# Four SwiGLU FFNs whose first product is made in seven block products of half the tokens instead of eight

## The reference, cut to what matters

```python
def swiglu_2(x, w_gate, w_up, w_down):
    return (jax.nn.silu(x @ w_gate) * (x @ w_up)) @ w_down
def second_block(...):
    for l in range(DEPTH_2):        # 2
        x = layer_norm(ALPHA * x + 0.5 * swiglu_2(x, ffn1_gate[l], ffn1_up[l], ffn1_down[l]), ...)
        ...                         # pooling and HGRN2 mixer, layer norm
        x = layer_norm(ALPHA * x + 0.5 * swiglu_2(x, ffn2_gate[l], ffn2_up[l], ffn2_down[l]), ...)
```

## Time and profile before

| | us |
|---|---|
| median of 3 runs | 2878.31 (2878.22 to 2878.59) |
| profiled execution, its span | 2877.4 |
| PE busy | 2850.9 (99%) |
| DVE busy | 1219.8 (42%) |
| ACT busy | 1009.8 (35%) |
| POOL busy | 398.4 (14%) |

### The profile page before, as it was taken

How to read it: one execution, slowest core, us unless ns; L and a number is a source line. 1 busy time by engine, 2 the same in 40 slices (tenths; PEclk the granted TensorE clock), 3 DMA queues, 4 the chain that set the end, 5 groups by cost and what they waited for, 6 DMA issues and landing times.

```text
span 2877.4 us, 34540 instructions
## 1 busy us (share of the span) xinstructions
PE 2850.9 (99%) x14629; PEld 2357.3 (82%) x14629; DVE 1219.8 (42%) x1631; ACT 1009.8 (35%) x1400; POOL 398.4 (14%) x422
## 2 busy tenths in 40 slices
PE   9999999899999999999999999999999999999999
PEld 8888887678888888888888888888888888888887
DVE  5554343553342433334646333343333464633333
ACT  5233244652232332323344323233222343432222
POOL 0115616201110000010232000100001013200010
PEclk9999999999999999999999999999999999999999
DMA  4333223123333233332212333323333221233332
GB/s 150 100 98 95 91 75 93 53 81 96 98 99 96 88 95 97 101 93 84 86 62 81 96 95 98 94 87 95 97 100 93 84 89 60 81 96 95 96 95 81
DMA packets 77465, 262.11 MB, mean 91 GB/s; under 512 B 12224, under 2 KB 12352, under 8 KB 77312
## 3 DMA queue, kind: packets, MB, share of 16 engines
q1 hardware_dynamic: 77312, 259.91, 29.1%
HBM read 256.60 MB, written 2.10 MB: 90 GB/s over the span
## 4 chain that ended last, share of the span: by engine, by line
PE 95%; DVE 2%; ACT 2%; issue 1%; POOL 0%; ACTq 0%; DVEq 0%; POOLq 0%
PE bank L340 26%; PE bank L342 25%; PE bank L341 25%; PE bank L357 2%; PE bank L363 2%; PE bank L358 2%; PE bank L477 2%; PE bank L406 1%; PE bank L410 1%; PE bank L407 1%; PE bank L487 1%; PE bank L377 1%; PE bank L373 1%; PE bank L372 1%; PE bank L799 1%
## 5 line engine op out<-in xcount | busy, mean ns | idle before, releaser
L1409 DVE TENSOR_TENSOR wlo<-wraw,whi 128x1024 fp32r<-128x1024 f32 x473 | 594.5, 1268 | 853.6 <-ACT whi L896 853.0
L896 ACT ACTIVATE whi<-wraw 128x1024 fp32r<-128x1024 f32 x478 | 499.9, 1056 | 929.5 <-DMA wraw<-weights 928.3
L340 PE MATMUL bank<-Hh,whi 128*128 128x512 f32 x2104 | 822.2, 391 | 2.3 <-DVE wlo L1409 1.1
L342 PE MATMUL bank<-Hl,whi 128*128 128x512 f32 x2104 | 818.9, 389 | 0.0
L341 PE MATMUL bank<-Hh,wlo 128*128 128x512 f32 x2104 | 818.7, 389 | 0.0
L340 PEld LDWEIGHTS bank<-Hh,whi 128*128 128x128 f32 x2104 | 395.0, 188 | 85.6 <-issue 3.1
L342 PEld LDWEIGHTS bank<-Hl,whi 128*128 128x128 f32 x2104 | 394.9, 188 | 82.1
L341 PEld LDWEIGHTS bank<-Hh,wlo 128*128 128x128 f32 x2104 | 395.1, 188 | 81.2
L340 PE MATMUL bank<-Ah,whi 128*128 128x512 f32 x1056 | 412.7, 391 | 0.0
L342 PE MATMUL bank<-Al,whi 128*128 128x512 f32 x1056 | 411.0, 389 | 0.0
L341 PE MATMUL bank<-Ah,wlo 128*128 128x512 f32 x1056 | 410.8, 389 | 0.0
(11 more groups left out here) (310 smaller groups left out, 2605.7 us busy)
## 6 DMA issues: line engine op xcount, KB each, us to landing
wraw<-weights SPq DMA_DIRECT2D x478, 512.0 KB, 3.6
X<-x_t SPq DMA_DIRECT2D x8, 256.0 KB, 6.5
y_t<-X SPq DMA_DIRECT2D x8, 256.0 KB, 2.1
dist<-attention SPq DMA_DIRECT2D x4, 256.0 KB, 4.2
wraw<-weights SPq DMA_DIRECT2D x2, 256.0 KB, 3.9
Y<-masks SPq DMA_DIRECT2D x1, 512.0 KB, 8.6
zsum<-attention SPq DMA_DIRECT2D x2, 256.0 KB, 3.3
MUb<-attention SPq DMA_DIRECT2D x2, 256.0 KB, 3.5
```

Of the source, the lines that this page charges most:

```text
L340: pe.matmul(b, sh, mh, start=start, stop=False)
L342: signal(pe.matmul(b, sh, ml, start=False, stop=stop), keys)
L896: act.activation(whi[:, u % NS, :], wraw[:, u % NS, :], ACT.Copy).then_inc(*S.done("weights_hi", ("hi", u)))
L1409: dve.tensor_tensor(wlo[:, u % NS, :], wraw[:, u % NS, :], f32(whi[:, u % NS, :]), SUB).then_inc(*S.done("weights_lo", ("lo", u)))
```

## The change

In the four FFNs with a layer norm, the first group (j = 0, 1) stays as it was. The other ten pairs go by 2x2 blocks: tokens in two halves a and b of 256, contraction in k and k+4, hidden tiles j and j+1. Instead of eight block products, seven are made, from sums of weight tiles and sums of token blocks, and each result block is a sum of some of them (the scheme of Strassen and Winograd). Gate and up are done alike, as the two halves e of one bank. In detail:

- The weights of these groups leave the stream. A step (a pair unit, v) is eight tiles, k and k+4 by j and j+1 by gate and up, loaded as 512 KB into one of four slots praw of 16 tiles. POOL adds up 512, 256 and 256 columns to make eight more tiles (`pair_sums`); ACT makes the high parts of 14 of the 16 (phi, three slots), DVE the low parts in place (plo).
- POOL makes four sums of token blocks for each of four k, once an FFN (`token_sums`); ACT and DVE split them into TF.
- PE does 7 x 2 x 3 matmuls of 256 columns a step, four steps a group, into seven banks.
- DVE adds the seven banks up to the four blocks in cb (`blocks`), ACT takes silu of the gate halves in one operation, DVE multiplies both hidden tiles in one (`product`) into Af, in float32, which lies where Al will.
- Slots and TF lie in the place of Ah from tile 4 on. So only tiles 0 to 3 are split early; the other 18 are split in `late_a`, when the last step is done, and there POOL makes a third of the Al. The first two units of the second product's weights are loaded behind the third-last step, the next two behind the last one (`behind`).
- One unit of each second-block mixer is blank and not loaded.

```diff
+FIRST_TILES = 4 * KD
+PAIRED = ("a0", "b0", "a1", "b1")
+N_PAIRS = (NF // 2 - 1) * 4
...
+KEPT = 4
...
+def pair_plan():
+    plan = []
+    for l in range(2):
+        for n in (1, 2):
+            for j in range(2, NF, 2):
+                for k in range(4):
+                    for kk, jj in ((k, j + 1), (k + 4, j + 1), (k, j), (k + 4, j)):
+                        plan.extend((f"{m}{n}_{l}", kk, jj) for m in ("gate", "up"))
...
+    Al, o_al = ar("Al", [P, NF, T], F32R)
+    Af, _ = ar("Af", [P, NF, T], F32, o_al)
+    Ah, o_ah = ar("Ah", [P, NF, T], F32R)
+    o_t = o_ah + KEPT * T * 4
...
+        def pair_group(st, j):
+            v0 = PAIRED.index(st) * N_PAIRS + (j - 2) * 2
...
+            for k in range(4):
+                v = v0 + k
+                raw, hi = pair_slots(v)
+                products = ((4, H[:, :, k, half[0]], None), (6, H[:, :, 4 + k, half[0]], None), (2, TF[:, :, 3, k, :], 3),
+                            (12, TF[:, :, 1, k, :], 1), (10, TF[:, :, 2, k, :], 2), (8, TF[:, :, 0, k, :], 0),
+                            (14, H[:, :, 4 + k, half[1]], None))
+                for i, (t, both, form) in enumerate(products):
+                    b = open_bank((use, i), True) if k == 0 else bank((use, i))
+                    if i == 0:
+                        pe.wait_ge(*S.at(("pair lo", v)))
+                    if form == 3 and j == 2:
+                        pe.wait_ge(*S.at(("TF", st, k)))
+                    if i == 3:
+                        pe.wait_ge(*S.at(("sum lo", v)))
+                    for e in range(2):
+                        o = b[:, half[e]]
+                        pe.matmul(o, plo[raw][:, t + e, :], both[:, 0, :], start=k == 0 and e == 0, stop=False,
+                                  skip_group_check=True)
+                        pe.matmul(o, phi[hi][:, t + e - 2, :], both[:, 0, :], start=False, stop=False,
+                                  skip_group_check=True)
+                        ins = pe.matmul(o, phi[hi][:, t + e - 2, :], both[:, 1, :], start=False, stop=k == 3,
+                                        skip_group_check=True)
...
+        def pair_hi(v):
+            raw, hi_slot = pair_slots(v)
+            s = v % N_PAIRS
...
+            act.wait_ge(pair_in[raw], 16 * pair_landings(v))
...
+                act.wait_ge(*S.at(("pair unit", v - 3)))
+            act.activation(phi[hi_slot][:, 0:6, :], praw[raw][:, 2:8, :], ACT.Copy).then_inc(
+                *S.done("weights_hi", ("pair hi", v)))
+            act.wait_ge(*S.at(("sums", v)))
+            act.activation(phi[hi_slot][:, 6:14, :], praw[raw][:, 8:16, :], ACT.Copy).then_inc(
+                *S.done("weights_hi", ("sum hi", v)))
...
+        def ffn_pairs(st, arena_free, tmp_free):
...
+            for k in range(4):
+                act.wait_ge(*S.at(("T sums", st, k)))
+                act.activation(TF[:, 0, :, k, :], Tf[:, :, k, :], ACT.Copy).then_inc(*S.done("moving_hi", ("TF hi", st, k)))
+            pair_hi(v0)
+            pair_hi(v0 + 1)
...
+            for j in range(2, NF, 2):
+                for k in range(4):
+                    s = 2 * (j - 2) + k
+                    if 0 < s < N_PAIRS - 2:
+                        pair_hi(v0 + s + 2)
+                    elif s >= N_PAIRS - 2:
+                        hi(u0 + 4 + s - N_PAIRS + 2)
+                    if k == 0 and j > 2:
+                        silu_pair(st, j - 2)
...
+                    if k == 3:
+                        act.wait_ge(*S.at(("full", ((st, j), 0))))
+                        act.wait_ge(*S.at(("product", st, j - 1)))
+                        act.activation(cb[:, 0, :], bank(((st, j), 0))[:, :], ACT.Copy).then_inc(
+                            *S.done("rows_out", ("first product", st, j), empties=[((st, j), 0)]))
...
+        def split_a(st, j):
+            act.wait_ge(*S.at(("product", st, j)))
+            act.activation(Ah[:, j, :], Af[:, j, :], ACT.Copy).then_inc(*S.done("moving_hi", ("Ah", st, j)))
+        def late_a(st):
...
+            for j in range(KEPT, NF):
+                hi_to(p + j)
+                if j == NF - 4:
+                    silu_pair(st, NF - 2)
+                split_a(st, j)
...
+        def pair_lo(v):
+            raw, hi_slot = pair_slots(v)
+            dve.wait_ge(*S.at(("pair hi", v)))
+            dve.wait_ge(*S.at(("sums", v)))
+            dve.tensor_tensor(plo[raw][:, 2:8, :], praw[raw][:, 2:8, :], f32(phi[hi_slot][:, 0:6, :]), SUB).then_inc(
+                *S.done("weights_lo", ("pair lo", v)))
+            dve.wait_ge(*S.at(("sum hi", v)))
+            dve.tensor_tensor(plo[raw][:, 8:16, :], praw[raw][:, 8:16, :], f32(phi[hi_slot][:, 6:14, :]), SUB).then_inc(
+                *S.done("weights_lo", ("sum lo", v)))
...
+            for k in range(4):
+                dve.wait_ge(*S.at(("TF hi", st, k)))
+                dve.tensor_tensor(TF[:, 1, :, k, :], Tf[:, :, k, :], f32(TF[:, 0, :, k, :]), SUB).then_inc(
+                    *S.done("moving_lo", ("TF", st, k)))
+            pair_lo(v0)
...
+            for j in range(2, NF, 2):
+                for k in range(4):
+                    s = 2 * (j - 2) + k
+                    if 0 < s < N_PAIRS - 2:
+                        pair_lo(v0 + s + 2)
+                    elif s >= N_PAIRS - 2:
+                        lo(u0 + 4 + s - N_PAIRS + 2)
+                    if k == 0 and j > 2:
+                        product(st, j - 2)
...
+                    if k == 3:
+                        blocks(st, j)
+        def blocks(st, j):
...
+            c11, c12, c21, c22, u2 = cb[:, 0, :], cb[:, 1, :], cb[:, 2, :], cb[:, 3, :], tmp[4][:, :]
+            dve.wait_ge(*S.at(("first product", st, j)))
+            dve.wait_ge(*S.at(("full", ((st, j), 3))))
+            dve.tensor_tensor(u2, b(3), c11, ADD).then_inc(*S.done("blocks", ("u2", st, j), empties=[((st, j), 3)]))
+            dve.wait_ge(*S.at(("u2", st, j)))
+            dve.tensor_tensor(c11, b(1), c11, ADD).then_inc(*S.done("blocks", ("c11", st, j), empties=[((st, j), 1)]))
+            dve.wait_ge(*S.at(("full", ((st, j), 4))))
+            dve.tensor_tensor(c21, b(4), u2, SUB).then_inc(*S.done("blocks", ("w", st, j)))
+            dve.wait_ge(*S.at(("w", st, j)))
+            dve.tensor_tensor(c21, b(2), c21, ADD).then_inc(*S.done("blocks", ("c21", st, j), empties=[((st, j), 2)]))
+            dve.wait_ge(*S.at(("full", ((st, j), 5))))
+            dve.tensor_tensor(c12, b(5), u2, ADD).then_inc(*S.done("blocks", ("u4", st, j), empties=[((st, j), 5)]))
+            dve.wait_ge(*S.at(("u4", st, j)))
+            dve.tensor_tensor(c22, b(4), c12, SUB).then_inc(*S.done("blocks", ("c22", st, j), empties=[((st, j), 4)]))
+            dve.wait_ge(*S.at(("full", ((st, j), 6))))
+            dve.wait_ge(*S.at(("c22", st, j)))
+            dve.tensor_tensor(c12, b(6), c12, ADD).then_inc(*S.done("blocks", ("blocks", st, j), empties=[((st, j), 6)]))
+        def product(st, j):
+            dve.wait_ge(*S.at(("silu", st, j)))
...
+            dve.tensor_tensor(Af[:, j:j + 2, :].rearrange("p j (h t) -> p (j h) t", h=2), cb[:, :, HALF:T], cb[:, :, 0:HALF],
+                              MUL).then_inc(*S.done("gates", ("product", st, j), ("product", st, j + 1), *last))
...
+        def late_a(st):
+            for j in range(KEPT, NF):
+                lo_to(p + j)
+                if j == NF - 4:
+                    product(st, NF - 2)
+                if j % 3:
+                    split_a(st, j)
...
+        def pair_sums(v):
+            raw = praw[pair_slots(v)[0]]
+            pool.wait_ge(pair_in[pair_slots(v)[0]], 16 * pair_landings(v))
+            pool.tensor_tensor(raw[:, 8:12, :].rearrange("p (f e) n -> p f (e n)", f=2),
+                               raw[:, 2:6, :].rearrange("p (f e) n -> p f (e n)", f=2),
+                               raw[:, 0:2, :].rearrange("p e n -> p (e n)").unsqueeze(1).to_broadcast([P, 2, 2 * P]),
+                               ADD).then_inc(*S.done("pool_pairs", ("two sums", v)))
+            pool.wait_ge(*S.at(("two sums", v)))
+            pool.tensor_tensor(raw[:, 12:14, :], raw[:, 8:10, :], raw[:, 4:6, :], ADD).then_inc(
+                *S.done("pool_pairs", ("third sum", v)))
+            pool.wait_ge(*S.at(("third sum", v)))
+            pool.tensor_tensor(raw[:, 14:16, :], raw[:, 12:14, :], raw[:, 6:8, :], ADD).then_inc(
+                *S.done("pool_pairs", ("sums", v)))
+        def token_sums(st):
+            a, b = slice(0, HALF), slice(HALF, T)
+            for k in range(4):
+                pool.wait_ge(*S.at(row_done(st, k)))
+                if k == 0:
+                    pool.wait_ge(*S.at(row_done(st, 4)))
+                pool.wait_ge(*S.at(row_done(st, 4 + k)))
+                pool.tensor_tensor(Tf[:, 2, k, :], X[:, k, b], X[:, 4 + k, b], SUB).then_inc(
+                    *S.done("pool_pairs", ("T third", st, k)))
+                pool.tensor_tensor(Tf[:, 0, k, :], X[:, k, a], X[:, k, b], SUB)
```

(29 more changed lines are left out.)

191 lines of the change are left out of this document (161 added, 30 removed).

## The result

The changed kernel takes 2987.07 us (median of four runs, 2985.11 to 2991.26), the kernel before 2878.26 on the same chip: ratio 1.038, interval 1.0366 to 1.0395. The forecast was 2890, with 2830 to 2945 as its range. The sign was the likelier one, the size was missed, and most of what was missed stands in a part that the prediction had put at nothing.

The account below looks back on a forecast made before the run. TensorE, busy 2850.9 of 2877.4 us, was taken as the bound, so only its work could be removed. Groups -42, FFN starts +24 and second products +30 gave +12: forecast 2890 us, eight-in-ten range 2830 to 2945.

Parts of the forecast that it names:

- Mixers: Second-block mixers: one unit each left blank, neither loaded nor read, forecast to cost nothing.
- Group: Forty changed groups: 20.7 us each instead of 21.76, 42 us won, ends 98 won and 6 lost.
- the pace: TensorE's 256-column matmuls in changed groups: taken as 0.1175 us each, between 0.113 and 0.120, so 19.74 us a group.
- the price of the lock: Changed groups: DVE's low parts and product exclude POOL's sums; locked work 18.4 to 20.8 us a group.
- The pace's floor of 0.110: TensorE in changed groups: weight loads keep the pace of matmuls from going under 0.110 us.
- Start of a changed FFN: After each changed FFN's first group: TensorE waits for token sums and splits, 6 x 4 = 24 us lost (4 to 36).
- Start of the second product: Four changed FFNs: 18 of 22 tiles split late, TensorE waits, 7.5 x 4 = 30 us lost (22 to 40).
- (c): Whole-kernel rival: lock whole, first sum at full price, block sums always late, group 22.2, total 2960 us; chance 0.14.
- If both are under 2 us the kernel is faster: Changed FFNs: waits of some 6 us after the start and 4 us in the second product; both under 2 reverses the sign.
- Half of each term's way to its end: Whole forecast: its own range, taken halfway to each term's end, stated as 2861 to 2930 us.
- Rows 8: Earlier profile's DVE and POOL pair: 8.72 us of work in 8.06, overlapped by 0.66 only; a pair takes some 2.23.
- Two thirds of the meetings: Changed FFN's start: with that share of DVE and POOL conflicts paid, the last token sum ends at 1948.4.

Follow-up runs that it names:

- e2: Kernel before with only the 12 blank tiles in each of the two second mixers, look-ahead positions unmoved: 2933.45 us, ratio 1.0194.
- e1: Changed kernel with ACT's and DVE's weight-split positions in the second mixers moved by the 12 blank tiles: 2953.78 us, ratio 1.0264.
- e10: Kernel before with the 12 blank tiles in each second mixer and the look-ahead positions moved by 12: 2890.01 us, ratio 1.0035.
- e3: Changed kernel with DVE's block sums and ACT's first-product copy ahead of the weight splits in a group's last step: 2945.12 us, ratio 1.0235.
- e11: Changed kernel with moved look-ahead, block sums first, early second-product splits, reordered FFN starts sharing token sums with DVE, earlier mixer splits: 2849.77 us, ratio 0.9900.

## Why the prediction was wrong, point by point

**The step that failed** is the last sentence ahead of the sum: "Mixers: one unit each is left blank and neither loaded nor read: nothing." It cost 59 us. e2 alone shows 55.6 with nothing else changed; e1 and e10 show by what: the positions of the splits in that stretch are written as constants behind the stage's start, the change moved the tiles by 12 and not the constants. The blank tiles were read as work that goes away; they are also a shift in a coordinate in which ACT's and DVE's look-ahead is written. The order of the program would have shown it: the tiles moved by one and a half units, and the places among ACT's and DVE's instructions where they are split did not move with them. Without these 59 us the kernel would be at some 2928, inside the range that was stated, with 30 and 13 us missed to one side and 8 to the other; that sum would have been right in part by luck.

**Group, -42 forecast, -12 measured.** Both its terms were small: the pace was 0.1201 and not 0.1175, 0.44 us a group and 17 us in all, at the upper end that was named; and the waits were 1.16 us a group, not 0.96, 8 us. The other 5 us are half clock behind the waits of two starts, which lies inside the segments. The mechanism was the one named, banks held until DVE's block sums. What was missed is that it was not the price of the lock that decided but the order: the work of DVE and POOL, from which 20.7 came, is the same in e3 and meets no less, and there a group takes 20.46. The pace's floor of 0.110 was laid to the weight load from two runs; the 128-column one is fp32, and at two passes its columns alone take 0.107, so only the 64-column run speaks for a load.

**Start of a changed FFN, +24 forecast, +16 measured.** Gaps of 5.8, 1.3, 8.2 and 2.0 us, released by the first step's low part, as described. The two short ones were short because the mixers were late: with these repaired (e1) they are 5.8, 8.3, 8.2 and 8.3, so the 6 us taken were a little low. That no half clock was added failed too: 6.8 and 10.2 us of it stand at the two long waits, and the matmuls at half pace behind them (27 and 25, at 0.214 us) lost 2.7 and 2.5 us, which the table has in the groups.

**Start of the second product, +30 forecast, +43 measured.** Step by step it went as written: the unit landed at T + 3.9 (3.8 forecast), the first Al at T + 6.8 (6.9), the wait 3.9 (4.2). Row 0 ended at T + 25.8, over the upper end of 24.5. 6.8 us of half clock stand in each of these products, 3.4 us of matmul time, which the sum had left out here altogether.

**Rivals.** None took place. The total is nearest to (c), 2960, but its mechanism, the lock whole and a group of 22.2 us, did not: a group took 21.46. The lock is as read from the earlier trace rows, partial.

**What would make it wrong.** "If both are under 2 us the kernel is faster" agrees with e11: no wait in its changed FFNs is over 2 us, and it is 1.0% faster than the kernel before.

**Slips in the working.** None moves the total. Half of each term's way to its end gives 2848 below and some 2925 above, not 2861 and 2930. Rows 8 give 0.33 us of overlap a pair, so 2.19 and not 2.23. Two thirds of the meetings put the last token sum at 1948.1, not 1948.4.

## What to carry to other kernels

When a layout edit inserts or drops tiles, list every place where a position is written as a number, and follow one weight unit through each engine's queue before and after it; an unloaded unit costs no transfer and still costs look-ahead. On an in-order engine, work that frees a bank goes ahead of work that waits for a third engine, even if the latter is needed first by count (42 us here, e3). And when TensorE waits several microseconds, price the wait with the matmuls behind it at the lower clock, and expect that taking away one wait uncovers the next.
